# Hybrid attention and MoE trunk, one core: the gate matmuls dealt to other attention units, and another semaphore ahead of eight score matmuls

## The reference

```python
hn = rmsnorm(h, norm_mix)
proj = hn @ w_in                      # q, k, v of all branches, branch gates, mg (2 x 1024)
o_a   = banded_attention(aq, ak, av, window=128, sinks)     # branch A
o_cmp, o_slc = nsa_compressed_selected(bq, ...)             # branches C and S
o_win = banded_attention(bq, bkw, bvw, window=512)          # branch W
o_b = gates0 * o_cmp + gates1 * o_slc + gates2 * o_win
g_a, g_b = split(sigmoid(mg), 2)
merged = g_a * (o_a @ w_br_a) + g_b * (o_b @ w_br_b)
h = h + merged @ w_out
h = h + hier_moe(rmsnorm(h, norm_ffn))                      # 32 experts, top 2
out = rmsnorm(h, norm_final)
```

## Time and profile before

| What | Value |
|---|---|
| median of 3 runs | 1729.42 us (1728.84 to 1729.5) |
| profiled execution, its own time | 1727.31 us |
| its span | 1725.5 us |
| PE busy | 1547.5 us, 90% of the span |
| DVE, ACT, POOL busy | 33%, 20%, 19% |
| mean granted TensorE clock | 0.968 of full speed |

### The profile page before, as it was taken

How to read it: one execution, slowest core, us unless ns; L and a number is a source line. 1 busy time by engine, 2 the same in 40 slices (tenths; PEclk the granted TensorE clock), 3 DMA queues, 4 the chain that set the end, 5 groups by cost and what they waited for, 6 DMA issues and landing times.

```text
span 1725.5 us, 21482 instructions
## 1 busy us (share of the span) xinstructions
PE 1547.5 (90%) x7541; PEld 833.4 (48%) x7542; DVE 563.7 (33%) x1519; ACT 348.8 (20%) x859; POOL 323.6 (19%) x464
## 2 busy tenths in 40 slices
PE   6999998898999898988899999299899999999980
PEld 3554543343444444444444455166466666666650
DVE  4210004665555645554223244411111111111107
ACT  3000003443333343333100111111111111111112
POOL 2000002332332323232000011312112212112113
PEclk9999999999999999999999999599999999999995
DMA  9114621543111010102252922469999999999937
GB/s 251 38 50 63 116 78 55 175 164 101 43 25 31 25 43 25 31 25 70 80 198 78 387 88 87 181 263 418 418 421 417 411 356 404 422 418 417 416 115 292
DMA packets 136008, 332.09 MB, mean 192 GB/s; under 512 B 39256, under 2 KB 79608, under 8 KB 126736
## 3 DMA queue, kind: packets, MB, share of 16 engines
q1 hardware_dynamic: 117472, 297.98, 47.3%
q0 software_dynamic: 10080, 21.32, 3.6%
q10 hardware_dynamic: 8400, 12.07, 2.0%
HBM read 276.08 MB, written 55.25 MB: 192 GB/s over the span
## 4 chain that ended last, share of the span: by engine, by line
PE 78%; DVE 7%; DMA 7%; issue 3%; ACT 2%; POOL 1%; SPq 1%; ACTq 0%; POOLq 0%; DVEq 0%
PE PS L785 15%; PE PS L673 11%; PE PS L562 10%; PE PS L799 8%; PE PS L704 6%; PE PS L739 6%; PE PS L620 4%; PE PS L659 4%; DMA WA<-w 4%; PE PS L639 3%; PE PS L557 3%; PE PS L763 1%; DVE mx L1066 1%; PE PS L544 1%; PE PS L608 1%
## 5 line engine op out<-in xcount | busy, mean ns | idle before, releaser
L673 PE MATMUL PS<-WA 128*128 128x512 f32 x512 | 261.4, 623 | 17.8 <-ACT WA L877 17.8
L785 PE MATMUL PS<-WA,BA 128*64 128x256 f32 x2048 | 231.7, 384 | 4.7 <-DMA WA<-w 3.6
L785 PEld LDWEIGHTS PS<-WA,BA 128*64 128x64 f32 x2048 | 175.1, 139 | 68.5 <-issue 20.2
L562 PE MATMUL PS<-WA,BA 128*128 128x512 f32 x416 | 181.8, 597 | 4.9 <-DVE WA L981 4.9
L1305 POOL TENSOR_SCALAR BA<-BA,rin,gates 128x640 f32<-128x640 f32 (+7 forms) x128 | 100.1, 782 | 300.9 <-DVE rin L1089 300.8
L673 PEld LDWEIGHTS PS<-WA 128*128 128x128 f32 x512 | 85.4, 191 | 110.4 <-issue 79.8
L1218 DVE SCALAR_TENSOR_TENSOR BA<-BA,PS 128x256 f32<-128x256 f32 x46 | 19.4, 422 | 359.9 <-ACT BA L924 359.9
L870 ACT ACTIVATE BA<-PS,ngm 128x640 f32<-128x640 f32 (+7 forms) x128 | 89.8, 702 | 219.8 <-DVE ngm L1067 219.6
L562 PEld LDWEIGHTS PS<-WA,BA 128*128 128x128 f32 x416 | 79.1, 191 | 102.9 <-issue 97.4
L639 PEld LDWEIGHTS PS<-ident,BA 128*128 128x128 f32 x648 | 80.7, 144 | 97.5 <-issue 64.7
L799 PE MATMUL PS<-WA,BA 128*64 128x512 f32 x512 | 116.9, 597 | 9.9 <-DVE BA L1228 8.3
(11 more groups left out here) (221 smaller groups left out, 1491.6 us busy)
## 6 DMA issues: line engine op xcount, KB each, us to landing
WA<-w SPq DMA_DIRECT2D x66, 2048.0 KB, 22.9
BA<-w SPq DMA_DIRECT2D x30, 2048.0 KB
rows_d<-WA SPq DMA_DIRECT2D x8, 2048.0 KB, 8.7
rows_d<-BA ACTq DMA_DIRECT2D x92, 128.0 KB
WA<-w_in SPq DMA_DIRECT2D x16, 512.0 KB, 5.3
gates_d<-WA SPq DMA_DIRECT2D x32, 256.0 KB, 2.4
WA<-gates_d SPq DMA_DIRECT2D x8, 1024.0 KB, 5.5
BA<-w_in SPq DMA_DIRECT2D x26, 256.0 KB, 5.4
```

Source lines behind the costliest of these rows:

```text
L562: mm = pe.matmul(PS[:, j % 4, :], ws[:, c % 6, k, :], hnT[:, k, 512 * h:512 * h + 512], start=(k == 0), stop=(k == KT - 1))
L673: mm = pe.matmul(PS[:, 6, :], gw[:, j, k, :], hnT[:, k, 512 * hf:512 * hf + 512], start=(k == 0), stop=(k == KT - 1))
L785: mm = pe.matmul(PS[DH * h:DH * h + DH, bank, 0:256], xT[:, k, :], w[par][:, k, 256 * h:256 * h + 256], start=(k == 0), stop=(k == KT - 1))
```

## The change

It has two parts. In the table of gate steps, a unit that opens a head pair now stops short of a tile's last step (`step_no % KT == KT - 1`), so tiles end in second units, in A or in C units. The dealing stops at a tile's end as before, so what is owed then goes to the next unit. In `scores`, where the unit just before is a C unit (the first W unit of each query tile), PE waits for the exponential of the unit ahead of C and for C's `front`, in place of C's exponential. Nothing is computed otherwise; the number of every instruction stays the same.

```diff
         here = []
-        while step_no < want and (not here or step_no % KT or n == NU - 5):
+        opens = u[1] in "WS" and u[2] < REP
+        while step_no < want and (not here or step_no % KT or n == NU - 5) and not (opens and step_no % KT == KT - 1):
             here.append(step_no)
             step_no += 1
@@ scores(u)
             if u >= 2:
-                pe.wait_ge(S["exp_done"], u if pair else u - 1)
+                freed = u if pair else u - 1
+                if units[freed - 1][1] == "C":
+                    pe.wait_ge(S["exp_done"], freed - 1)
+                    pe.wait_ge(S["front"], freed)
+                else:
+                    pe.wait_ge(S["exp_done"], freed)
```

## The result

The changed kernel takes 1734.87 us in the median of 10 runs (1731.18 to 1737.89), against 1729.46 us for the kernel before (median of 10). The ratio is 1.0028, with a 95% interval of 1.0019 to 1.0037: it is slower by about 5 us. The prediction was 1732 us, within 1721 to 1740.

A forecast was written before the change was run, and what follows sets the result against it. PE, busy 90% of the span, bounds the kernel; only its idle time and clock can change. Terms 8.5 - 4.8 - 2.8 + 1.7 = +2.6 us on 1727.31, plus 2.1 for the median, give 1732 us, range 1721 to 1740.

The forecast's parts named there:

- the clock terms: Half clock avoided behind C of i = 4, -2.8 us; one new half-clock stretch at an emptied pair, +1.7 us.
- part two: First W scores behind C start 0.66 us sooner at seven places, 0.17 at i = 3: -4.8 us.
- part one: Tiles ending in first units: 31 steps move to later units at 0.86 us each, less returned waits: +8.5 us.
- the waits simply go: Rival: tanh waits in attention come back as time, postponed steps find slack; 25 us at most, 1713 us if half; chance 0.14.
- The clock falls more often: Rival: emptied pairs drop PE to half clock in three or more places, 1741 us; chance 0.22.
- Part one costs nothing: Rival: moved gate steps land where PE waits anyway, only -4.8 and -2.8 us remain, 1722 us; chance 0.12.
- The rule from the Trainium skill: Short PE idle times between matmul groups make its clock swing between two levels; by it the change would lose.
- the tanh waits: Sign: PE's gate-step waits for ACT's tanh in attention fall from 17.8 to about 5 us.
- the pair of four first-unit steps: Sign: the pair behind the emptied one takes about 8.4 us from scores to scores.
- The waits of the pair scores for the exponential: Sign: in attention these PE waits rise from 16.6 us by 10 us or more.
- the clock was not full at i = 4: Sign: behind C of i = 4, PE was forecast to run at full clock after the change.
- the pair with the 1.57 us tanh wait: Pair at 599.80 us, taking 6.98 us: its exponential sets a 5.88 us floor, so at most 1.1 us returns.

The follow-up runs named there:

- tiles_only: The kernel before with only the new tile-end condition in the table of gate steps, keeping the old wait behind C: 1739.82 us, ratio 1.0061.
- cwait_only: The kernel before with only the new wait behind C, keeping the old table of gate steps: 1721.21 us, ratio 0.9949.
- changed_again: The changed kernel run once more, unaltered, in a second series against the kernel before: 1734.16 us, ratio 1.0030.
- owed_in_second: The changed kernel, but units that open a pair take only steps falling due there; owed steps go to second units: 1727.76 us, ratio 0.9987.

## Why the prediction was right, and where it was not

**The direction and the size.** The forecast was a small loss, 1732 us; it is 1734.87 us. The reason given was that a pair's length is set by the chain from its scores over the old transposes and DVE's copy to the second exponential, that a gate step in a first unit lengthens this chain and one in a second unit does not, and that the change moves steps into first units. The experiments show this from both sides, with the same steps in each pair: 58 steps moved into first units cost 36 us, 32 moved into second units give 6 to 7 us, and with the link cut the changed kernel's own table gives 10 us back. The number was 2.9 us low: the clock terms were 1.1 us that should have been nothing, part two was 0.6 us too large, part one about 0.7 us too small, and the rest lies within the scatter of the runs (the second series stands 4.5 us above before, not 5.4).

**Part one, +8.5 us.** Measured alone +10 us, of which nothing is a higher share of half clock (0.9665 in both kernels). The pairs came out as worked out: 5.87 and 8.41 us for 5.88 and 8.41. Added up place by place between the traces of before and of `tiles_only`, without the pair whose clock had fallen before, the ten places from i = 4 on cost 7.2 us (7.3 predicted) and the six with i up to 3 cost 2.0 us (1.2 predicted). The term was mis-sized at i = 2, where three places cost 0.5 to 0.6 us each and not 0.1 to 0.3.

**Part two, -4.8 us.** The term was 0.1 us too large at each place, since PE started 0.15 us behind the end of DVE's subtraction. In the trace of `cwait_only` the six places behind C of i = 1, 2 and 4 to 7 start their scores 0.56 to 0.58 us sooner each, and that of i = 3 0.25 us. With as much at i = 0 this makes 4.2 us. Alone the part gave 9 us, some 3 us of which go with the higher clock of that kernel's runs. Which place of the program that clock is owed to was not settled.

**The clock, -2.8 and then +1.7 us.** These two terms failed as I put them. I read one execution's fall as the effect of the old wait. At the place behind C of i = 4 the changed kernel still fell to half clock in both profiles, for the tail of the scores and the steps, and the pair took 9.30 us. `tiles_only`, with the old wait, stayed at full clock there (7.73 us), and so did `cwait_only`, with the new one (7.70 us). Over the eleven profiles of this case the clock fell there in six. So the size that I took was right (2.8 us for 3.0), and its cause was wrong. The profile of the changed kernel had four falls in attention, ahead of the tail, that the one of before did not have. But `changed_again` had only two falls ahead of the tail, as many as the one of before, and over 12 runs the mean clock was no lower than before. The net of my two terms, -1.1 us, should have been taken as 0 with an uncertainty of some microseconds. With part two at 4.2 us and no clock term the sum is 8.5 - 4.2 = +4.3 us on 1729.46 us, that is 1733.8 us; measured are 1734.2 and 1734.9.

**The rivals.** That the waits simply go was wrong for the reason given: they turned into waits for the exponential (16.6 to 25.1 us). "The clock falls more often" was true of the profiled execution, 9.5 us over before, and not of the median. "Part one costs nothing" is excluded by `tiles_only`. The rule from the Trainium skill (TensorE: Matmul & The Clock Gate, "A second HAM failure mode: psum-queue depth-cycling") has in this case's traces one row for it and one against it: the fall behind the emptied pair at 605 us, and the same pair in `changed_again` without a fall. These falls did not decide between the two kernels.

**The signs.** Of the signs that the prediction named, the tanh waits (5.8 us) and the pair of four first-unit steps (8.41 us) came as said. The waits of the pair scores for the exponential rose by 8.5 us, a little less than the 10 us named, and the clock was not full at i = 4.

**What I did not see.** The prediction had all that was needed for the better table, since it said that a second-unit step is free while PE waits. It did not draw the conclusion that the kernel before already had 99 of its 256 steps in first units. Nor did it ask whether pairs that keep PE busy throughout should hold steps at all. A table that mends both gave 33 us, many times what the change was about.

## What to carry to other kernels

A filler that an in-order engine does beside a chain is free only where it does not stand ahead of something the chain needs. Look at what is queued behind it, not at how much idle time the engine has. Ask too whether the engine has room there at all: of the 33 us that the better table gave, 19.4 us came at eight pairs in which PE was already busy throughout and which lost 23 steps. The change itself removed 12 us of tanh waits and ended 5 us slower. And read what a removed wait is worth from the next wait behind it: the pair with the 1.57 us tanh wait could give back only 1.1 us.

## What the runs showed of the hardware

A profile is one draw of the clock. In two profiled executions of the changed kernel the clock fell five times and twice ahead of the tail of attention, and only the fall behind C of i = 4 came in both, though their scores up to 390 us started within 0.1 us of each other. Single executions of one kernel differed by up to 12.6 us (`owed_in_second`, 1721.73 us at 0.972 and 1734.31 us at 0.964), mostly in step with the mean clock, so a difference of 5 us is not read from one execution of each; the two profiles of the changed kernel differ by 5.7 us themselves (spans of 1735.0 and 1729.3 us). The fall at 608 us came behind a stretch in which PE was partly busy, 1.19 of 3.30 us from 605 us. PE had not stood still throughout, and in `changed_again` the same pair was followed by no fall.

Behind C of i = 4, PE's scores started 0.15 us after the end of the DVE instruction that they waited for (504.92 to 505.07).
